# Feed-forward up panels as seven block products in chunks 1 to 7

## The reference, cut to what matters

```
D_FF = 4 * D_MODEL                      # D_MODEL = 1024, SEQ = 512, DEPTH = 2
for layer in range(DEPTH):
    ...
    h = h + y
    y = _rms_norm(h, mlp_norm_g[layer])
    h = h + jnp.square(jax.nn.relu(y @ w_up[layer])) @ w_down[layer]
return _rms_norm(h, final_norm_g)
```

## Time and profile before

| what | value |
|---|---|
| median of 3 runs | 2160.33 us (2159.52 to 2160.78) |
| span of the profiled execution | 2157.4 us; no time of its own is given beside it, so the median of the runs stands for it, 2.9 us more |
| busy share of the span | PE 99%, PEld 82%, DVE 54%, ACT 41%, POOL 45% |
| feed-forward, layer 0 | first up panel at 1151.65 us, last down panel ends at 1500.7 us |
| feed-forward, layer 1 | first up panel at 1790.93 us, last down panel ends at about 2143 us |

### The profile page before, as it was taken

One profiled execution on the slowest core, in us unless ns is written; L12 is line 12 of the kernel. 1 busy time (PEld: TensorE's weight loads), 2 busy tenths in 40 slices (PEclk: granted clock), 3 DMA queues, 4 the chain that ended last, 5 costly groups with the idle time before them and its releaser, 6 DMA issues.

```text
span 2157.4 us, 29579 instructions
## 1 busy us (share of the span) xinstructions
PE 2132.0 (99%) x10318; PEld 1776.3 (82%) x10318; DVE 1167.1 (54%) x1715; ACT 892.1 (41%) x1321; POOL 966.0 (45%) x707
## 2 busy tenths in 40 slices
PE   9999999999999999999999999999999999999998
PEld 7888888778888888878888888888788887888886
DVE  7655556887777777787355222224565565222223
ACT  5433233555655555455534223224345444233223
POOL 4443535355444444316445445444443325444443
PEclk9999999999999999999999999999999999999999
DMA  6232222232222222223222222224212212222221
GB/s 225 87 103 83 97 83 78 89 137 98 79 78 78 84 91 78 104 82 117 98 78 98 98 96 85 98 97 130 98 63 75 79 59 79 98 97 97 97 97 59
DMA packets 38416, 202.09 MB, mean 94 GB/s; under 512 B 4395, under 2 KB 9643, under 8 KB 16076
## 3 DMA queue, kind: packets, MB, share of 16 engines
q1 hardware_dynamic: 29504, 191.46, 25.2%
q10 hardware_dynamic: 8844, 9.70, 1.5%
HBM read 195.90 MB, written 5.24 MB: 93 GB/s over the span
## 4 chain that ended last, share of the span: by engine, by line
PE 89%; DVE 6%; issue 2%; DVEq 2%; ACT 1%; POOL 0%; DMA 0%; POOLq 0%; SPq 0%; ACTq 0%
PE bank L450 15%; PE bank L451 15%; PE bank L456 15%; PE bank L437 12%; PE bank L438 12%; PE bank L439 12%; DVE SS L1799 1%; PE bank L970 1%; PE bank L490 1%; DVE X L2022 1%; PE bank L732 1%; PE bank L491 1%; PE bank L495 1%; DVE T L2019 1%; ACT WH L1126 1%
## 5 line engine op out<-in xcount | busy, mean ns | idle before, releaser
L368 POOL TENSOR_TENSOR WL<-RAW,WH 128x512 fp32r<-128x512 f32 x700 | 959.8, 1402 | 1162.6 <-ACT WH L1126 1162.6
L1126 ACT ACTIVATE WH<-RAW 128x2048 fp32r<-128x2048 f32 (+1 forms) x190 | 337.2, 1777 | 591.3 <-PE bank L439 288.1
L450 PE MATMUL bank<-HH,WH 128*128 128x512 f32 x968 | 382.7, 395 | 0.8 <-DVEq L2353 0.8
L451 PE MATMUL bank<-HL,WH 128*128 128x512 f32 x968 | 377.3, 390 | 0.0
L456 PE MATMUL bank<-HH,WL 128*128 128x512 f32 x968 | 241.5, 391 | 0.0
L450 PEld LDWEIGHTS bank<-HH,WH 128*128 128x128 f32 x968 | 181.8, 188 | 39.9 <-DVEq L2353 1.0
L456 PEld LDWEIGHTS bank<-HH,WL 128*128 128x128 f32 x968 | 181.6, 188 | 39.9 <-issue 2.4
L451 PEld LDWEIGHTS bank<-HL,WH 128*128 128x128 f32 x968 | 181.9, 188 | 37.7 <-issue 1.0
L2319 DVE TENSOR_TENSOR X<-X,bank 128x512 f32<-128x512 f32 x128 | 87.6, 686 | 193.7 <-PE bank L456 117.5
L2310 DVE SCALAR_TENSOR_TENSOR TG<-bank,RS 128x512 f32<-128x512 f32 x64 | 44.0, 688 | 206.9 <-PE bank L439 135.8
L437 PE MATMUL bank<-HH,WH 128*128 128x512 f32 x288 | 112.2, 390 | 0.7 <-DVE HL L1788 0.7
(11 more groups left out here) (440 smaller groups left out, 4364.7 us busy)
## 6 DMA issues: line engine op xcount, KB each, us to landing
RAW<-panels SPq DMA_DIRECT2D x174, 1024.0 KB, 4.8
X<-xin SPq DMA_DIRECT2D x4, 512.0 KB, 7.6
xsave<-X ACTq DMA_DIRECT2D x4, 512.0 KB, 2.8
X<-xsave ACTq DMA_DIRECT2D x1, 2048.0 KB, 13.7
TAB<-scratch ACTq DMA_DIRECT2D x16, 128.0 KB, 3.1
out<-ACC SPq DMA_DIRECT2D x8, 256.0 KB, 2.3
RAW<-panels SPq DMA_DIRECT2D x2, 512.0 KB, 6.6
T<-xtok SPq DMA_DIRECT2D x2, 512.0 KB, 12.7
```

The lines of the kernel that those rows point to most:

```text
L368: gp.tensor_tensor(WL[:, s, cs], RAW[:, s, cs], WH[:, s, cs].bitcast(f32), ALU.subtract).then_inc(lo_ready, 1)
L450: nc.tensor.matmul(o, wh[:, columns[k - k0]], xh[:, k, :], start=first and k == k0, stop=False)
L451: nc.tensor.matmul(o, wh[:, columns[k - k0]], xl[:, k, :], start=False, stop=False)
L1126: return nc.scalar.activation(dst, src, ACT.Copy)
```

## The change

The up panels of chunks 1 to 7 are computed by a scheme with seven block products in place of eight. A panel (1024 input channels x 256 hidden units) is cut into four blocks of 512 x 128, the input HH, HL into four quarters of 512 channels x 256 tokens. Of the seven left factors three are blocks of the panel (`weights`), three are sums of blocks (`sums`, tiles WSH, WSL), and one is a difference that takes the place of the fourth block; of the right factors three are sums of input quarters (XTH, XTL), one is a sum written over the quarter HH[:, 0:4, 256:512], and three are quarters as they are. Each product is 4 blocks x 3 matmuls of 256 columns. They go to half banks; ACT copies intermediate states of them to R and SS, and DVE puts the outputs together from copies and banks.

Chunk 0 keeps its panels, and the input sums are made during it: on DVE `x_sums` in front of its first relu, on ACT three splits between hidden tiles 1 and 2 and one behind tile 3, on DVE three subtractions between HIDL 1 and relu 2. ACT's split of the first down panel in chunk 0 moves behind hidden tile 0. From chunk 1 on TensorE no longer takes the next chunk's first up panel in the same turn of its loop, and down tiles go to banks 0 to 7 in order. POOL subtracts seven pieces of 512 columns for such a panel. On the host the 14 up panels of a layer that this concerns are laid out by blocks. The rest of the program is as it was, except that some semaphores are shared between stages.

```diff
+            def seven_products(c, L, j, n, s, banks):
+                p = seven(c, L, j)
+                def product(o, wh, wl, x, first, sig, value):
+                    for k in range(4):
+                        ks = slice(128 * k, 128 * k + 128)
+                        nc.tensor.matmul(o, wh[:, ks], x(0, k), start=first and k == 0, stop=False, skip_group_check=True)
+                        nc.tensor.matmul(o, wh[:, ks], x(1, k), start=False, stop=False, skip_group_check=True)
+                    pe.wait_ge(sig, value)
+                    for k in range(4):
+                        ks = slice(128 * k, 128 * k + 128)
+                        end = nc.tensor.matmul(o, wl[:, ks], x(0, k), start=False, stop=k == 3, skip_group_check=True)
+                    return end
...
+                pe.wait_ge(S["seven_hi"], 3 * p + 1)
+                o0 = bank(banks[0])[:, 0:256]
+                product(o0, *weights(0), quarter(0, 0), True, lo_ready, 4 * n + 1).then_inc(S["seven_made"], 1)
+                o3 = bank(banks[3])[:, 0:256]
+                product(o3, *weights(2), quarter(1, 0), True, lo_ready, 4 * n + 2).then_inc(S["seven_made"], 1)
+                o2 = bank(banks[2])[:, 0:256]
+                product(o2, *weights(1), combined(2), True, lo_ready, 4 * n + 3).then_inc(S["seven_made"], 1)
+                pe.wait_ge(S["seven_hi"], 3 * p + 2)
+                o1 = bank(banks[1])[:, 0:256]
+                product(o1, *sums(0), combined(0), True, S["seven_lo"], 3 * p + 1).then_inc(S["seven_made"], 1)
+                pe.wait_ge(S["seven_copied"], 3 * p + 1)
+                product(o0, *sums(1), combined(1), False, S["seven_lo"], 3 * p + 2).then_inc(S["seven_made"], 1)
+                pe.wait_ge(S["seven_copied"], 3 * p + 2)
+                pe.wait_ge(S["seven_hi"], 3 * p + 3)
+                product(o1, *sums(2), quarter(1, 1), False, S["seven_lo"], 3 * p + 3).then_inc(S["seven_made"], 1)
+                pe.wait_ge(S["seven_copied"], 3 * p + 3)
+                pe.wait_ge(hi_ready, n + 1)
+                product(o0, *weights(3), quarter(0, 1), False, lo_ready, 4 * n + 4).then_inc(panel_used, 1)
...
                 first_panel(n0)
                 if L == 0:
                     sum_of_squares(name)
...
+                second_panel(L == 1)
+                down_panels(0, (4, 5, 6, 7, 0, 1, 2, 3))
+                pe.wait_ge(S["norm_h_split"], COMBINED[L] + 4)
+                with pe.Fori(1, CHUNKS) as c:
+                    uses.loop(c, [2] * 8, first=1)
+                    seven_products(c, L, 0, c * 4 + n0, n0 % 2, (0, 1, 2, 3))
+                    seven_products(c, L, 1, c * 4 + (n0 + 1), (n0 + 1) % 2, (4, 5, 6, 7))
+                    down_panels(c, range(8))
```

On ACT (`high_direct` splits three blocks, `high_first_sums` two sums, `high_last_sums` one sum and the difference, `copy_of` copies 256 columns from PSUM):

```diff
+                def first_chunk():
+                    hidden(0, 0)
+                    split_at(n0 + 2)
+                    hidden(0, 1)
+                    for i, t in ((0, ACC[:, 0:4, 0:256]), (1, ACC[:, 4:8, 256:512]), (2, ACC[:, 4:8, 0:256])):
+                        act.wait_ge(S["x_sums"], 4 * L + (2, 3, 4)[i])
+                        hi(XTH[:, i], t).then_inc(S["norm_hi"], 1)
+                    hidden(0, 2)
+                    split_at(n0 + 3)
+                    hidden(0, 3)
...
                 def chunk(c, last=False):
+                    high_direct(c, 1)
+                    copy_of(c, 0, 0)
+                    high_first_sums(c, 1)
+                    copy_of(c, 0, 2)
+                    high_last_sums(c, 1)
+                    copy_of(c, 0, 1)
+                    copy_of(c, 0, 3)
+                    hidden(c, 0)
+                    copy_of(c, 1, 0)
+                    hidden(c, 1)
+                    split_in(c, 4, n0 + 2)
+                    copy_of(c, 1, 2)
+                    copy_of(c, 1, 1)
+                    copy_of(c, 1, 3)
+                    hidden(c, 2)
+                    hidden(c, 3)
+                    split_in(c, 4, n0 + 3)
...
                     if not last:
-                        split_in(c, 4, n0 + 4)
-                        split_in(c, 4, n0 + 5)
+                        high_direct(c + 1, 0)
+                        high_first_sums(c + 1, 0)
+                        high_last_sums(c + 1, 0)
```

On DVE (`weight_sums` makes the four sums of a panel's blocks, 512 columns each; `outputs` four results of 256 columns and two relus):

```diff
+                def x_sums():
+                    q = [[ACC[:, 4 * i:4 * i + 4, 256 * t:256 * t + 256] for t in range(2)] for i in range(2)]
+                    for k in range(KD):
+                        v.tensor_scalar(ACC[:, k, :], X[:, k, :], gain(f"mlp{L}", k), None, ALU.mult)
+                    ve.drain()
+                    v.tensor_tensor(q[0][0], q[0][1], q[0][0], ALU.subtract)
+                    v.tensor_tensor(q[0][1], q[1][1], q[0][1], ALU.subtract).then_inc(S["x_sums"], 1)
+                    ve.drain().then_inc(S["x_sums"], 1)
+                    v.tensor_tensor(q[1][1], q[1][1], q[0][0], ALU.subtract)
+                    ve.drain().then_inc(S["x_sums"], 1)
+                    v.tensor_tensor(q[1][0], q[1][1], q[1][0], ALU.subtract)
+                    ve.drain().then_inc(S["x_sums"], 1)
...
+                def first_chunk():
+                    x_sums()
                     for j in range(2):
                         for f in range(2 * j, 2 * j + 2):
+                            tile_done(ve, "mlp_up_made", f, 2, n0 + f // 2, 0, 2 * L)
+                            rectified(0, f, B[f][:, :]).then_inc(S["mlp_relu"], 1)
                             ve.drain().then_inc(free[f], 1)
+                        low_hidden(0, j)
+                        if j == 0:
+                            for i in range(3):
+                                low_x_sum(i)
+                            ve.drain()
+                    low_x_sum(3)
+                    ve.drain()
+                    weight_sums(1, 0)
                     for f in range(KD):
+                        tile_added(0, f, (f + 4) % 8, False)
+                        if f == 4:
+                            weight_sums(1, 1)
+
+                def chunk(c, last):
+                    outputs(c, 0)
+                    low_hidden(c, 0)
+                    outputs(c, 1)
+                    low_hidden(c, 1)
+                    if not last:
+                        weight_sums(c + 1, 0)
+                    for f in range(KD):
+                        tile_added(c, f, f, last)
+                        if f == 4 and not last:
+                            weight_sums(c + 1, 1)
```

More of the change, by code:

```diff
@@ L27 @@
 PARTS = 4
+BLOCK = PANEL // 4
 N_RET = 0
@@ L908, in other_panels @@
                             inverse_rows_of_tokens(4, 4)
[L909 to L919, removed]
                 first_panel(n0)
@@ L923, in mlp @@
                     sum_of_squares(name)
[L924 to L932, removed]
+                second_panel(L == 1)
[6 more added lines that the diff above has]
+                    down_panels(c, range(8))
+                uses.end(CHUNKS - 1)
             mlp(0, N_MLP0)
@@ L1619, in chunk @@
                     if last and L == 0:
                         act.wait_ge(S["rows_stored"], 64)
[L1621 to L1630, removed]
@@ L1631, in chunk @@
-                    if not last:
-                        split_in(c, 4, n0 + 4)
-                        split_in(c, 4, n0 + 5)
-                with act.Fori(0, CHUNKS - 1) as c:
+                        for kind in range(4):
+                            bias_table(kind)
+                    if not last:
+                        high_direct(c + 1, 0)
+                        high_first_sums(c + 1, 0)
+                        high_last_sums(c + 1, 0)
+                first_chunk()
+                with act.Fori(1, CHUNKS - 1) as c:
@@ L2301, in mlp, with rectified, low_hidden @@
                 at = 4 * CHUNKS * L
-                def chunk(c, last):
+                def rectified(c, f, src):
+                    if f >= 2:
+                        ve.wait_ge(S["mlp_hid_f32"], c * 4 + (at + f - 1))
+                    return v.scalar_tensor_tensor(TG[:, f % 2, :], src, 0.0, RS[:, :], ALU.max, ALU.mult)
+                def low_hidden(c, j):
+                    for f in range(2 * j, 2 * j + 2):
+                        ve.wait_ge(S["mlp_hid_hi"], c * 4 + (at + f + 1))
+                        lo(HIDL[:, f, :], T[:, f, :], HIDH[:, f, :]).then_inc(S["mlp_hid_split"], 1)
@@ new lines, in tile_added @@
+                def tile_added(c, f, b, last):
+                    tile_done(ve, "mlp_down_made", f, 4, c * 4 + (n0 + 2 + f // 4), c * 6, 6 * CHUNKS * L)
+                    end = v.tensor_tensor(X[:, f, :], X[:, f, :], B[b][:, :], ALU.add)
+                    if last:
+                        end.then_inc(S["x_updated"], 1)
+                        ve.drain().then_inc(free[b], 1)
+                        if L == 0 and f > 0:
+                            gained("mix1", f - 1)
+                        if L == 1 and f > 1:
+                            add_square("final", f - 1)
+                    else:
+                        end.then_inc(free[b], 1)
```

225 lines of the change are left out of this document (173 added, 52 removed).

## The result

The changed kernel takes **2183.91 us** (median of 4 runs, 2182.93 to 2188.4), the kernel before 2160.2 in the same comparison: a ratio of 1.0112, 95% interval [1.0098, 1.0127]. It is slower, as forecast, but by 24 us where 5 were forecast, and 3.9 us above the range's upper end.

A forecast was written before the change was run, and what follows sets the result against it. TensorE, busy in 99% of the span, was taken as the bound. -23.2 + (10.8 to 13.3) + (12.5 to 15.0) + 1 + 1 = +2.1 to +7.1 gave 2165 us; own range 2160 to 2171, with rivals 2154 to 2180.

The forecast's parts named there:

- Block products, 23.2 us: Up panels of chunks 1 to 7: 84 matmuls of 0.1196 us take 10.05 us, 0.83 less; 28 panels save 23.2 us.
- (a): Up panels: 256-column matmuls take under 0.1196 us because repeated weights shrink their fixed part; 2154 us; chance 0.25.
- (d): Up panels: 84 weight loads of 0.19 us one after another, 16 us a panel; about 2310 us; chance 0.03.
- No stall in a running chunk, 0.5 us of room: Running chunks: ACT's copy for the second accumulator is the tightest place, ready 0.5 us early; no stall charged.
- (b): Up panels: PSUM copies on ACT come late behind a split, half a microsecond a panel, 14 us; 2179 us; chance 0.12.
- The heads, 10.8 to 13.3 and 12.5 to 15.0: Chunk 0 of layers 0 and 1: input sums ahead of the first relu delay the down panels by these us.
- Nothing gives this back: After chunk 0: its loss stays and chunk 1 adds none, POOL's first subtractions being some 5 us early.
- the 1 us for register instructions: Running chunks: register instructions in front of waits, charged 1 us in all.
- Clock, +1: After the holes in chunk 0: stretches of half clock on TensorE, charged 1 us in all, ends 0 and 6.4.
- a chunk that isn't 41.9 us: Chunks 1 to 7: any length other than 41.9 us would show the forecast wrong, pointing to (a) or (b).
- a first hole under 6: Ahead of the first down panel: a hole under 6 us, where about 8 and 9 were forecast, would show it wrong.
- The third: TensorE's granted clock below 1 for more than a stretch after each hole would show the forecast wrong.

The follow-up runs named there:

- Moving the sums: Kernel of 2163.5 us with chunk 0's input-sum products and differences moved from ahead of the first relu to other places on VectorE: 2146.8 us.
- the trim: Kernel of 2146.8 us with the second panel's weight sums ahead of addition 4 and, in layer 1, three gain products and the first difference earlier: 2140.95 us.
- the kernel with the split first: Kernel of 2166.46 us with chunk 0's split of the first down panel put back ahead of the first hidden tile on ScalarE: 2163.5 us.
- the halves exchanged: Changed kernel with the two halves of the banks swapped in chunks 1 to 7, first attention units still in banks 6 and 7: 2166.46 us.

## Why the prediction was right and wrong

- *Block products, 23.2 us.* Right in mechanism and nearly in size: 1.58 us a chunk make 22.1. A panel is 10.08 us, 0.12 a matmul, the upper end that was kept. Rivals (a) and (d) are out. So is the gap formula of the Trainium skill (TensorE: Matmul & The Clock Gate, Back-to-back issue gap), by which 256 columns are an estimated 109 ns: the trace has 120.
- *No stall in a running chunk, 0.5 us of room.* Right: 41.94 us without a gap, 0.7 us of room in the trace, and holes once it is used up. Rival (b) is out.
- *The heads, 10.8 to 13.3 and 12.5 to 15.0.* Right: 12.5 in layer 0; 15.4 in layer 1, 0.4 over the stated end, though the terms themselves (9.6 + 4.4 + 1.4; in layer 0 7.9 + 4.4 + 1.4) add up to 15.4 and 13.7, not to 15.0 and 13.3. The holes are 7.2 us (7.9 said) ended by POOL's WL and 1.6 ended by HIDL (2.4 to 4.4 said), 9.2 and 2.2 in layer 1. The first is shorter partly because the eight products took 3.26 us and not 3.9, the second because the half clock (1176.83 to 1187.07 in layer 0) stretched the work ahead of it, as the prediction had it. Moving the sums, with the trim behind it, gave 16.7 and 5.9 us back.
- *The step that failed: "Nothing gives this back; nor does chunk 1 add to it, since by the same count POOL has the first subtractions of its first panel some 5 us before TensorE gets there".* The count followed the data of chunk 1 and not the banks. The chunks with block products write banks 0 to 7 in order; chunk 0 leaves them in the order 4 to 7, 0 to 3. The banks that it empties last are the first to be wanted, and their additions stood behind four sums at up to 1.8 us. Charged at nothing, it was 11.0 us.
- *The same at the other end, not mentioned at all.* The last chunk leaves tiles 6 and 7 in the banks of the first attention units: 8.1 us. With both seams mended the kernel takes 2166.46, where 2165 was forecast; so the seams are the whole error but for a microsecond or two. That 2165 is met so closely is in part luck: the products saved 1.1 us less than forecast and the heads cost 2.1 more than their middle (12.5 + 15.4 for 25.8), while the stage began 0.7 earlier and the 1 us for register instructions does not show in a running chunk.
- *Clock, +1.* About right for the heads, whose losses above contain it. The seams and the tail brought more, which the prediction did not count: some 1.5 us behind the first seam in each layer, 1.3 behind the second, and 1.4 in the tail, where the clock fell earlier.

Two of the signs that the prediction named for being wrong (a chunk that isn't 41.9 us, a first hole under 6) did not show. The third did: TensorE was at half clock for 6.0 us behind the first hole of layer 0 (1181.06 to 1187.07) and 4.7 in layer 1, more than one stretch of 3.41. But the heads' losses above contain it, so it is not what made the forecast wrong. All three looked at places that the prediction had counted.

## What to carry to other kernels

A loop in steady state says nothing about its seams: when the order of PSUM banks changes in a loop, follow each bank over the first and the last turn, from the engine that empties it (with all that is queued ahead of that) to the product that wants it next. Where the first turn is written out by hand, the loop should take over its order of banks. And preparation that is put at the head of a stage is to be placed in the idle time of its engine before the stage or behind the first result: here that was worth 22.6 us, as much as the block products save (22.1).

## What was not expected of the hardware

VectorE and GpSimd slow each other by the operands. Two lines of the changed kernel, one line of the code each, and the page's group of the additions, which read one operand from PSUM:

```profile
L2506 DVE TENSOR_TENSOR ACC<-RAW x28: 1772/1776/1781, 1198.0 to 2120.5; 128x512 f32<-128x512 f32 x28
...
L2508 DVE TENSOR_TENSOR ACC<-ACC,RAW x28: 693/1618/1624, 1199.8 to 2122.4; 128x512 f32<-128x512 f32 x28
...
L2490 DVE TENSOR_TENSOR X<-X,bank 128x512 f32<-128x512 f32 x128 | 80.5, 682 | 20.0 <-PE bank L502 10.0
```

A sum of two operands in SBUF takes 0.69 us alone and 1.6 to 1.8 behind a subtraction of GpSimd. Which of the two starts first decides: nine of the 28 first sums of a panel (L2505) began ahead of GpSimd's next subtraction, some by less than 0.1 us, and took 0.69, and it was the subtraction that then took 1.5 to 1.8 us instead of 1.3. An addition from a bank takes 0.68 on the mean of 128 and never over 0.69, though GpSimd was at work beside 112 of them, so it is not slowed; and the product with a gain, with a single SBUF operand, 0.48 us alone and 1.3 to 1.5 beside GpSimd (three of the eight that took 6.14 us instead of 3.26 in the kernel with the split first; the other five stayed at 0.48). The Trainium skill (SBUF — State Buffer, SBUF: two separate sides) has a rule for this: VectorE's operations with two SBUF inputs, or in a mode that uses two ports, and GpSimd's take turns at a shared pair of ports: the one that starts first holds it for its whole length, and the other waits. The trace agrees for the sums and for the additions from a bank; for the product it agrees if that runs in such a mode, which no run here shows. The prediction had more than doubled the subtractions (2.0 to 2.3 us measured, 1.2 alone) and left the products at 0.48, which held only as long as GpSimd had nothing to do beside them.

Second, the clock: half clock follows holes, but not each of them, and not the same ones in executions of nearly the same list. In layer 1 of the changed kernel the hole of 2.2 us was followed by 3.4 us of it, in layer 0 the one of 1.6 us by none; with the halves exchanged it was layer 0's (2.7 us) and not layer 1's (1.9). A hole filled with useless matmuls kept the clock there and won nothing in the end.
